# A two-layer recurrent trunk on one core: the recurrent unit inside layer 1's projections, first units tile by tile, last group by column halves, block B's scan a group later, 1/rms by ln and exp

## What is computed

```
layer 0 (even): gated linear attention (4 heads) beside retention (4 heads), as scans over chunks
layer 1 (odd):  mLSTM (4 heads) beside a recurrent unit of 512 channels:
    xc = bias + sum of 4 taps of rx over time           (causal convolution)
    r, i = sigmoid(block-diagonal W_r xc), sigmoid(W_i xc)
    a = exp(-8 r softplus(-lam));  u = sqrt(1 - a^2) * i * xc
    h_t = a_t h_{t-1} + u_t;  output = h * gelu(gate)
```

## Time and profile before

| | us |
|---|---|
| median of 3 runs | 2603.36 (2598.88 to 2606.93) |
| the profiled execution | 2599.3 |
| its span, first to last instruction | 2597.3 |
| TensorE matmuls busy | 2480.4 (95%) |
| VectorE, ScalarE, GpSimd busy | 1056.5, 903.6, 1266.8 |
| mean granted TensorE clock | 0.976 of full speed |

### The profile page before, as it was taken

One profiled execution on the slowest core, in us unless ns is written; L12 is line 12 of the kernel. 1 busy time (PEld: TensorE's weight loads), 2 busy tenths in 40 slices (PEclk: granted clock), 3 DMA queues, 4 the chain that ended last, 5 costly groups with the idle time before them and its releaser, 6 DMA issues.

```text
span 2597.3 us, 36699 instructions
## 1 busy us (share of the span) xinstructions
PE 2480.4 (95%) x15562; PEld 2217.9 (85%) x15562; DVE 1056.5 (41%) x1691; ACT 903.6 (35%) x1182; POOL 1266.8 (49%) x674
## 2 busy tenths in 40 slices
PE   7999998899999999999989899999978999999997
PEld 5889986688787888999979889988866779999997
DVE  3523245344335521544664451154475345222224
ACT  4332344342223412433444241344444223222222
POOL 5645454645545744533534474344342536544554
PEclk9999998999999999999989999999998999999999
DMA  4222233123232232222212222222222223222222
GB/s 161 90 79 73 74 124 102 62 77 110 90 105 81 92 97 97 74 82 82 90 49 90 74 92 94 93 90 73 86 74 96 84 98 122 90 90 91 88 90 82
DMA packets 72322, 233.17 MB, mean 90 GB/s; under 512 B 8768, under 2 KB 10848, under 8 KB 72160
## 3 DMA queue, kind: packets, MB, share of 16 engines
q1 hardware_dynamic: 72160, 230.82, 26.9%
HBM read 221.74 MB, written 9.05 MB: 89 GB/s over the span
## 4 chain that ended last, share of the span: by engine, by line
PE 80%; DVE 7%; ACT 3%; issue 3%; POOLq 2%; POOL 2%; DVEq 1%; DMA 1%; SPq 0%; ACTq 0%
PE ps L670 56%; PE ps L700 17%; POOLq L1172 2%; DMA wr<-in_wblk 1%; DVE xc L1682 1%; POOL wl L1166 1%; ACT wh L954 1%; DVE mixl L1508 1%; PE ps L759 1%; PE ps L757 1%; PE ps L763 1%; DVE sq L1315 1%; DVE vm L1705 0%; DVEq L1522 0%; POOL rsB L1178 0%
## 5 line engine op out<-in xcount | busy, mean ns | idle before, releaser
L1166 POOL TENSOR_TENSOR wl<-wr,wh 128x1024 fp32r<-128x1024 f32 (+2 forms) x396 | 950.6, 2411 | 619.9 <-ACT wh L954 619.1
L670 PE MATMUL ps<-xh,wh 128*128 128x260 f32 (+3 forms) x3312 | 896.5, 325 | 26.4 <-DVE xl L1328 14.8
L670 PE MATMUL ps<-xh,wl 128*128 128x260 f32 (+3 forms) x3312 | 881.7, 321 | 0.0
L670 PE MATMUL ps<-xl,wh 128*128 128x260 f32 (+3 forms) x3312 | 881.6, 321 | 0.0
L670 PEld LDWEIGHTS ps<-xh,wh 128*128 128x128 f32 (+1 forms) x3312 | 550.7, 189 | 90.8 <-issue 44.5
L670 PEld LDWEIGHTS ps<-xh,wl 128*128 128x128 f32 (+1 forms) x3312 | 549.3, 188 | 48.0 <-issue 2.0
L670 PEld LDWEIGHTS ps<-xl,wh 128*128 128x128 f32 (+1 forms) x3312 | 549.5, 189 | 45.7 <-issue 1.9
L954 ACT ACTIVATE wh<-wr 128x1024 fp32r<-128x1024 f32 (+2 forms) x396 | 409.5, 1044 | 481.7 <-DMA wr<-in_wblk 478.0
L700 PE MATMUL ps<-hidh,wh 128*128 128x260 f32 (+1 forms) x1056 | 289.4, 328 | 34.9 <-DVE hf L1529 13.5
L700 PE MATMUL ps<-hidl,wh 128*128 128x260 f32 (+1 forms) x1056 | 285.7, 325 | 0.0
L700 PE MATMUL ps<-hidh,wl 128*128 128x260 f32 (+1 forms) x1056 | 284.7, 324 | 0.0
(11 more groups left out here) (326 smaller groups left out, 2219.2 us busy)
## 6 DMA issues: line engine op xcount, KB each, us to landing
wr<-in_wblk SPq DMA_DIRECT2D x392, 512.0 KB, 3.7
xr<-in_xT SPq DMA_DIRECT2D x8, 260.0 KB, 5.8
xB<-in_xT SPq DMA_DIRECT2D x8, 260.0 KB, 4.5
out_yT<-xB SPq DMA_DIRECT2D x8, 260.0 KB, 2.2
xr<-in_xT SPq DMA_DIRECT2D x8, 256.0 KB, 5.8
xA<-in_xT SPq DMA_DIRECT2D x8, 256.0 KB, 4.3
Ss<-in_s_even SPq DMA_DIRECT2D x1, 2048.0 KB, 9.9
out_ss_even<-Ss SPq DMA_DIRECT2D x1, 2048.0 KB, 9.3
```

What stands on the lines that cost most here:

```text
L670: mm = pe.matmul(ps[0:cols, b + c, 0:n], wt[:, w], xt[:, e:e + n], start=first, stop=end)
L1166: pool.tensor_tensor(wl[n % 4][:, 0:w], wr[n % 4][:, 0:w], wh[n % 4][:, 0:w].bitcast(F32), ALU.subtract).then_inc(s_lo, 1)
```

## The change

- **Recurrent unit.** `recurrent(X)` places it in layer 1's projections of the same block. The projection's columns are reordered (`IN1`): first the unit's input and gate tiles, then the rest. The convolution of tile j stands after projection 2 + 4j, its two gate matmuls after 4 + 4j, the first half of the rest after 5 + 4j, the second after 6 + 4j. Its buffers are shared by both blocks; its softplus of lam is made at the first convolution. Loads of its weights and states (`rgA`, `rgB`) and writes of its outputs (`rgout`) move with it.
- **Scan of block B in layer 0.** Its decay matmuls (`z`), log sums (`lg`), rotations (`rot`) and the load of B's residual (`xB`) move from before the feed-forward of A, and from its groups 0 and 1, to groups 0 to 2; its chunks begin at group 3 instead of 1, its samples and mixed tiles follow.
- **Scan of A's mLSTM** takes every second group; mixed tiles stand in group 10. The samples of layer 1 start in group 7 instead of 8.
- **1/rms** is exp(-0.5 ln(sum / 1024 + eps)), two activations of ScalarE straight from PSUM; the scaling and the reciprocal on VectorE go.
- **Start.** Parameters and x tiles are loaded first, the low parts of the first three weight blocks are made by VectorE, and the first two units (`sm` and the first projection) go side by side, tile of x by tile of x (`first_units`). The squares of these tiles are made after all splits and added by VectorE.
- **End.** The last "down" round of B runs in two halves of 260 columns (`dh`, one bank each); norm, scaling and writes of a half follow it (`xe`, `ne`, `fe`), the first half's within the second. The last two squared tiles go into the norm's sum on TensorE, not on GpSimd.

```diff
+IN1 = (12, 13, 14, 15, 20, 21, 22, 23, 0, 1, 2, 3, 4, 5, 6, 7, 8, 9, 10, 11, 16, 17, 18, 19)
...
+        if halves:
+
+            for c in range(2):
+                for m in range(KT):
+                    add(("dh", c, X, m))
+                    if m:
+                        add(("xe", c, m - 1))
+                    if c and m == 2:
+                        add(("ne", 0))
+                    if c and m == 4:
+                        add(("fe", 0))
+                add(("xe", c, KT - 1))
+            add(("ne", 1))
+            add(("fe", 1))
+            return
...
-    def scan(kind, X):
+    def scan(kind, X, places):
+
         at = {}
         for c in range(NC):
-            at[1 + c, 2] = [(kind, X, c, 0)]
-            at[1 + c, 4] = [(kind, X, c, 1)]
-            at[2 + c, 0] = [(kind, X, c, 2)]
-        at[1 + NC, 2] = [(kind, X, NC, 0)]
+            for ph in range(3):
+                g, q = places[ph]
+                at.setdefault((g + places[3][c], q), []).append((kind, X, c, ph))
+        at.setdefault((places[0][0] + places[3][NC], places[0][1]), []).append((kind, X, NC, 0))
         return at
...
     add(("dma", "start"))
-    add(("dma", "x0"))
+    add(("w", 0))
     for m in range(KT):
-        add(("xs", 0, m))
+        add(("dma", "x0", m))
+        add(("x0", m))
+        if m == 1:
+            add(("w", 1))
+    add(("w", 2))
+    add(("dma", "const"))
+    add(("w", 3))
+    for m in range(KT):
+        add(("q0x", m))
     add(("nrv", 0))
     add(("sm", 0, A))
     for j in range(24):
@@ -169,54 +195,53 @@
...
-    add(("dma", "xB"))
-    add(("dma", "retB"))
-    add(("z", B, 0))
-    add(("z", B, 1))
-    add(("nrm", 2))
-    add(("nrv", 2))
-    ffn(0, A, 3, merge({(0, 0): [("rot", B, 0)], (0, 1): [("rot", B, 1)], (0, 2): [("rot", B, 2)],
-                        (0, 3): [("rot", B, 3), ("lg", B, 0)], (1, 0): [("lg", B, 1)], (1, 1): [("s0i", B)]},
...
-    def rg_at(X, places):
-        at = {places[0]: [("rc", X, 0)]}
+    ffn(0, A, 3, merge({(0, 3): [("z", B, 0), ("z", B, 1), ("dma", "retB")],
+                        (1, 0): [("lg", B, 0)], (1, 1): [("lg", B, 1), ("rot", B, 0)], (1, 2): [("rot", B, 1)],
+                        (1, 3): [("rot", B, 2)], (2, 0): [("rot", B, 3)], (2, 1): [("s0i", B)], (2, 3): [("dma", "xB")]},
+                       scan("s0", B, ((0, 0), (0, 2), (0, 4), (3, 4, 5, 6, 7))),
+                       {(7, 1): [("dma", "smp0")], (7, 2): [("q0",)]},
+                       {p: [("qs", 2 * i), ("qs", 2 * i + 1)] for i, p in enumerate(((8, 0), (8, 2), (9, 0), (9, 2)))},
+                       {(9, 3): [("qe", 0)], (9, 4): [("qe", 1), ("dma", "smp0out")], (10, 0): [("qe", 2)],
+                        (10, 1): mix(0, B)[0:2], (10, 2): mix(0, B)[2:4], (10, 3): mix(0, B)[4:6], (10, 4): mix(0, B)[6:8]}))
+    out(0, B, 4, {2: [("nrm", 3), ("nrv", 3), ("dma", "rgA")]})
+
+    def projections(X, n, at):
+
+        add(("sm", 1, X))
+        for i, j in enumerate(IN1):
+            add(("in", 1, X, j))
+            if i == 0:
+                add(("nrm", n))
+                add(("nrv", n))
+            for s in at.get(i, ()):
+                add(s)
+        return
+
+    def recurrent(X):
+        at = {}
         for j in range(4):
-            at.setdefault(places[1 + j], []).extend([("rg", X, j, 0), ("rg", X, j, 1)] +
-                                                    ([("rc", X, j + 1)] if j < 3 else []) + [("ru", X, j)])
+            at.setdefault(2 + 4 * j, []).append(("rc", X, j))
+            at.setdefault(4 + 4 * j, []).extend([("rg", X, j, 0), ("rg", X, j, 1)])
+            at.setdefault(5 + 4 * j, []).append(("ru", X, j, 0))
...
         return {(0, 0): [("r1", X, 0)], (0, 1): [("r1", X, 1)], (0, 2): [("r1", X, 2)], (1, 0): [("p1", X)]}
-    ffn(0, B, 5, merge(rows(A), scan("s1", A), {(5, 3): [("dma", "rgA")]},
-                       rg_at(A, [(6, 0), (6, 2), (7, 0), (7, 2), (8, 0)]),
-                       {(9, 0): mix(1, A)[0:2], (9, 1): mix(1, A)[2:4], (9, 2): mix(1, A)[4:6], (9, 3): mix(1, A)[6:8]}))
+    projections(A, 4, recurrent(A))
+    ffn(0, B, 5, merge(rows(A), scan("s1", A, ((0, 2), (0, 4), (1, 1), (1, 3, 5, 7, 9))),
+                       {(10, 0): mix(1, A)[0:2], (10, 1): mix(1, A)[2:4], (10, 2): mix(1, A)[4:6], (10, 3): mix(1, A)[6:8]}))
     out(1, A, 6, {2: [("nrm", 5), ("nrv", 5)]})
-    for j in range(25):
...
     add(("dma", "oddB"))
-    ffn(1, A, 7, merge(rows(B), scan("s1", B), {(5, 3): [("dma", "rgB")]},
-                       rg_at(B, [(6, 0), (6, 1), (6, 3), (7, 1), (7, 3)]),
-                       {(6, 2): [("u0",)], (7, 0): [("u1",)], (7, 4): [("dma", "smp1")]},
-                       {p: [("us", 2 * i), ("us", 2 * i + 1)] for i, p in enumerate(((8, 3), (9, 1), (9, 3), (10, 0)))},
-                       {(10, 1): [("ue", 0), ("dma", "smp1out")], (10, 2): [("ue", 1)], (10, 3): mix(1, B)[0:4],
-                        (10, 4): mix(1, B)[4:8]}))
+    add(("dma", "rgout"))
+    ffn(1, A, 7, merge(rows(B), scan("s1", B, ((0, 2), (0, 4), (1, 0), (1, 2, 3, 4, 5))),
+                       {(6, 1): [("dma", "smp1")], (6, 2): [("u0",)], (7, 0): [("u1",)]},
+                       {p: [("us", 2 * i), ("us", 2 * i + 1)] for i, p in enumerate(((7, 2), (8, 0), (8, 2), (9, 0)))},
+                       {(9, 1): [("ue", 0), ("dma", "smp1out")], (9, 2): [("ue", 1)], (10, 0): mix(1, B)[0:2],
+                        (10, 1): mix(1, B)[2:4], (10, 2): mix(1, B)[4:6], (10, 3): mix(1, B)[6:8]}))
     out(1, B, 8, {2: [("nrm", 7), ("nrv", 7)], 3: [("fin", A)]})
-    ffn(1, B, 9, {})
-    add(("nrm", 9))
-    add(("nrv", 9))
-    add(("fin", B))
+    ffn(1, B, 9, {}, halves=True)
     return it
 
 
...
+                elif name == "rgA":
+                    sp.wait_ge(s_unit, pl.done(("down", 0, A, NG - 1, KT - 1)))
+                    sp.dma_start(wrg[:], a["wrg"]).then_inc(s_rgc[A], 16)
+                elif name == "rgB":
+                    sp.wait_ge(s_unit, pl.done(("down", 0, B, NG - 1, KT - 1)))
+                    sp.wait_ge(s_acc, KT * 6)
+                    sp.dma_start(wrg[:], a["wrg"]).then_inc(s_rgc[B], 16)
+                    sp.dma_start(h0[:], a["h0"]).then_inc(s_rgc[B], 16)
+                    sp.dma_start(cvi[:], a["conv"]).then_inc(s_rgc[B], 16)
...
+            def first_units(u):
+
+                started.add(0)
+                sh, sl = split_of(0)
+                for k in range(KT):
+                    for i, cols in ((0, small_cols(0)), (1, P)):
+                        if k == 0 and i == 0:
+                            x_tile_ready(0, 0)
+                            weights_ready(u)
+                        if k == 0 and i == 1:
+                            continue
+                        if k == 1 and i == 1:
+                            weights_ready(u + 1)
+                        if i == 0 and k:
+                            x_tile_ready(0, k)
+                        for kk in ((0, 1) if k == 1 and i == 1 else (k,)):
+                            w = slice(kk * cols, (kk + 1) * cols)
+                            e = slice(kk * W[A], (kk + 1) * W[A])
+                            for wt, xt, first, end in ((wh[i], sh, kk == 0, False), (wh[i], sl, False, False),
+                                                       (wl[i], sh, False, kk == KT - 1)):
+                                mm = pe.matmul(ps[0:cols, pl.bank[u + i], 0:W[A]], wt[:, w], xt[:, e], start=first, stop=end)
+                        if k == KT - 1:
+                            mm.then_inc(s_unit, 1)
 
             def on_x(u, X, n, cols):
...
+            def norm_half(c):
+                e = slice(260 * c, 260 * c + 260)
+                pe.wait_ge(s_acce, 6 * (c + 1))
+                pe.matmul(ps[:, 6 + c, 0:260], ones, rs[B][:, e], start=True, stop=False)
+                for m in (6, 7):
+                    pe.wait_ge(s_sqe, KT * c + m + 1)
+                    mm = pe.matmul(ps[:, 6 + c, 0:260], ones, sq[m % 2][:, e], start=False, stop=m == 7)
+                mm.then_inc(s_nrme, 1)
...
+            def norm_half(c):
+                e = slice(260 * c, 260 * c + 260)
+                act.wait_ge(s_nrme, c + 1)
+                act.activation(rs[B][:, e], ps[:, 6 + c, 0:260], ACT.Ln, bias=pcol("eps"), scale=1.0 / D)
+                act.drain()
+                act.activation(rs[B][:, e], rs[B][:, e], ACT.Exp, scale=-0.5).then_inc(s_rse, 1)
...
             def norm(n):
                 X = NORMS[n][0]
-                act.wait_ge(s_ne, n + 1)
-                act.activation(rs[X][:], rs[X][:], ACT.Sqrt).then_inc(s_nq, 1)
+                act.wait_ge(s_nrm, n + 1)
+                act.activation(cut(rs[X][:], X), bank(6, X), ACT.Ln, bias=pcol("eps"), scale=1.0 / D)
+                act.drain()
+                act.activation(rs[X][:], rs[X][:], ACT.Exp, scale=-0.5).then_inc(s_nq, 1)
...
-            def recurrent_unit(X, j):
+            def recurrent_unit(X, j, part):
+                w = W[X]
                 act.drain()
```

(47 more changed lines are left out.)

347 lines of the change are left out of this document (228 added, 119 removed).

## The result

The changed kernel takes 2540.97 us, median of 4 runs (2538.05 to 2543.01), against 2601.35 (2598.88 to 2606.93) for the kernel before on the same chip. The ratio is 0.9778, 95% interval 0.9765 to 0.9792. It is 2.2% faster. The forecast of 2530 was 11 us too low, inside its range. The profiled execution has a span of 2538.6 us, 58.7 less than the 2597.3 of before, where the prediction's terms add up to 73.2 less.

A forecast was written before the change was run, and what follows sets the result against it. The prediction took TensorE work as 80% of the chain of waits, so only its stands could earn time; the terms -24.8 - 16.1 - 22.5 - 2.3 - 4 - 3.5 = -73.2 us gave 2530 from the median 2603.36, range 2506 to 2560.

The forecast's parts named there:

- the likeliest case: Whole kernel: the forecast's own sum of terms holds, 2512 to 2550 us; chance 65 in 100.
- the unit's two lines: Recurrent unit out of the feed-forward: A's, counted with lambda, -27.1 us, and B's, -16.1 us.
- 1, recurrent unit, A: Feed-forward B of layer 0 sheds 26.8 us, layer 1's projections A lose 2: net -24.8 us (-18 to -26.8).
- 1, recurrent unit, B: Feed-forward A of layer 1 sheds 33.1 us, layer 1's projections B lose 17: net -16.1 us (-6 to -28).
- The rival of convolutions of 10.85 us: Layer 1's projections B: stops near 27 us, and the scan's start saves only 14; about 2554 us, 2 in 10.
- 2, the scan: Block B's scan in layer 0 a group later: 27 us lost there, 4.5 kept as lost, net -22.5 us (-14 to -26).
- the 9.8 us: Start of block B's scan: TensorE's wait for GpSimd's products, 9.8 us in one piece, claimed to go whole.
- 3, ln and exp, lambda: Norms between start and end count 0, two table loads taken; lambda work before A's mLSTM scan -2.3 us (0 to -3).
- 4, the start: First units tile by tile: TensorE stands 4 us, second projection near 27 us against 31.1; -4 us (0 to -9).
- 5, the end: Last group by halves: 13.5 us instead of 17.2 from TensorE's last unit to the end; -3.5 us (0 to -7).

The follow-up runs named there:

- s1: Changed kernel with GpSimd's whole start piece of block B's scan one A unit later, (2, 1) to (2, 2): 2531.73 us, ratio 0.9742.
- s3: Changed kernel with only the first products of GpSimd's start piece moved to (2, 2), memsets and state scaling staying at (2, 1): 2536.96 us, ratio 0.9762.
- s2: Changed kernel with only the eight transfers of x for block B moved from group 2 to group 4: 2537.90 us, ratio 0.9765.
- s4: Changed kernel with only block B's layer 0 scan, samples, mixed tiles and x transfers back at the places of the kernel before: 2543.52 us, ratio 0.9792.
- the last run: Changed kernel with scan start piece and B's convolutions moved one unit, first-half end scalings last, layer 0 samples and mixed tiles one place earlier: 2521.08 us, ratio 0.9718.
- n0: Changed kernel with nine norms back to VectorE scaling, ScalarE square root and VectorE reciprocal; the end's half norms keep ln and exp: 2539.97 us, ratio 0.9793.
- f1: Changed kernel with the end's first-half scalings moved behind the last accumulation of the second half on VectorE: 2536.59 us, ratio 0.9761.

## Why the prediction was right and where it failed

**Direction and size.** The time is in the range and the likeliest case came true: TensorE's stands around the recurrent unit went, and the projections took it up at a modest price. That the sum came so near is partly luck. The scan's term (3.9) fell far outside its own bounds (14 to 26), and a third of what it lacked was made up by the unit's two lines, 6.7 us better than forecast.

**1, recurrent unit, A.** Predicted 2 us lost in the projections beyond the gate matmuls; measured none: 144.32 less 137.06 is 7.26, the eight gate matmuls (7.3). The convolutions took 3.0 to 5.1 us where 5 was taken, and none was late. Feed-forward B of layer 0 came to 417.35 where 417 was named, clock 1.00.

**1, recurrent unit, B.** The projections came to 167.9 where 171 was named: 13.9 us lost beyond the gate matmuls (167.89 - 144.87 - 9.1) against 17. The mechanism was the forecast one, evacuations behind the convolution and the sigmoid behind the gelu. The convolutions took 3.8 to 8.2 us, where 8 was taken for all. The rival of convolutions of 10.85 us fell; its other half, a scan worth only 14 us, was nearer than the forecast.

**2, the scan, the step that failed.** The prediction said "so the 9.8 us goes whole". The score matmul's wait did go whole, and the sentence stopped there. It asked whether the products still come in time, and not what stands behind the ten microseconds of GpSimd that make them. At the new place that is a gate's multiplication with VectorE, ScalarE and a weight block in a row behind it. The stop came back as 8.4 us. s1 and s3 move the piece against that multiplication, whole and in part, and get back 9.4 and 3.4 us in their stages. The transfers of x, which the prediction did price, cost nothing (s2). Where the prediction looked, it saw rightly: from output projection A to the start of group 2 the time fell from 136.46 us to 108.56. The rest is that the work moved on and met other things. What else is short of -22.5, some 18.6 - 9.4 = 9.2 us, lies in small stops behind that place. The largest part is in group 10 with its last "down" units, where the mixed tiles now stand, in the changed kernel and before:

```profile
794.71:848.25 53.54, 45.80 (x195) 35.74 (x194) 35.20 (x39) 24.86 (x34) 27.72 (x14) 1.00 0.28 91
```

```profile
809.80:857.62 47.82, 45.13 (x193) 35.59 (x192) 19.06 (x25) 16.17 (x21) 25.82 (x13) 1.00 0.28 90
```

With the items back at their old places (s4) it takes 48.2 us, so these 5.7 us come with the placement. The one edit tried there (the last run) left 52.5 us and gave nothing in its stage; which item costs them stays open.

**3, ln and exp, lambda.** The norms are hidden, as counted (n0); lambda gave 2.2 us of 2.3 by the traces, and no run has it alone. Ln followed by Exp takes two table loads; at the end of the changed kernel on ScalarE:

```profile
2527.76 1.28 ACT L1099 ACT_TABLE_LOAD   x1
2530.29 0.48 ACT L1099 ACTIVATE rsB<-ps,par 128x260 f32<-128x260 f32 x1 [1.25 <-PE ps L799]
2530.82 1.28 ACT L1101 ACT_TABLE_LOAD   x1
```

The first load is made while ScalarE waits for the norm matmul and costs nothing, the second stands on the path. The Trainium skill (ScalarE: Activation LUTs, "Table sets: the hidden batching unit") says that ln then exp need one load. This trace does not agree: it has two, of 1.28 us each, as the prediction took.

**4, the start.** -3.9 against -4. TensorE stood 2.57 us where 4 were forecast. The norm matmul ran at 25.13 us (24.5 forecast) and the second projection began at 25.66 (27), 5.5 us earlier than before. Then its 7.44 us, for 5.44, ran at a granted clock of 0.77, which is the 2 us that the forecast had put ahead of it. The hit is good to 2 us only: in the other runs the same start ended between 157.6 and 160.0 us, 3.4 to 5.8 less than before.

**5, the end.** Forecast 13.5 us from TensorE's last unit to the end, measured 16.7. The queue of scalings ahead of the last accumulations was forecast, and its length was one term mis-sized: 8 x 0.38 was taken, and they took 4.77 us. The second half's eight, with no sum of GpSimd beside them, took 3.29; the first half's have three beside them. The other term is what comes behind the last accumulation, up to the end of the Exp: 3.9 was taken, and it took 5.9 us (2526.63 to 2532.53). The norm matmuls, behind the stand of 5.3 us, ran at a granted clock of 0.50, the lower level of 1.2 GHz, the first half's at 1.00 (2.4 GHz), 2.97 us against 1.12. In f1, behind a stand of 2.7 us, the same six ran at 0.87 and took 1.69. Windows of the two, the second half's and the first half's:

```profile
2527.28:2530.25 2.97, 2.97 (x6) 1.85 (x6) 0.00 (x0) 1.70 (x2) 0.00 (x0) 0.50 0.03 8
...
2516.89:2518.01 1.12, 1.12 (x8) 0.97 (x7) 0.43 (x1) 1.10 (x2) 0.96 (x2) 1.00 0.00 0
```

## What to carry to other kernels

When a wait goes, look at the engine that was waited for: its work has only moved, and at its new place something else stands behind it in that engine's order. Ask of each long piece what the next item on that engine is and who waits for it. Here ten microseconds of GpSimd cost TensorE 8.4 us ahead of a gate's multiplication, and no stop of 2 us right behind it.

And read an edit worth a few microseconds from the stage that it touches. The span of the whole kernel put 3.8 us of another stage's wandering into the gain of s1.

## Unexpected of the hardware

A tap of VectorE on one to eight columns takes 0.21 to 0.22 us alone and up to 2.43 us when it meets a GpSimd rounding of 2.41 us; one on 511 columns takes 0.75 us alone and 2.71 when it meets one. So how often VectorE's taps meet a rounding counts, more than their size. The same code in the same place varies by 5 us (164.1 to 169.1), and the slower four of the seven are those where the third convolution met two roundings. That is more than several edits here were worth.
